# Ten chained transformer sublayers on one core: the last two output slots written token half by token half, the next input prepared in tile pairs, and unused matmuls while TensorE waits at each layer boundary

## What is computed

```python
def first_block(x, c, ...):               # sublayers 0 to 3
    for i in range(2):
        shift, scale, gate = ada_modulation(c, ada_w[i, 0], ada_b[i, 0])
        h = x * (1.0 + scale) + shift
        y = windowed_gqa(h, ...) if i == 0 else recurrent_block(h, ...)   # sublayers 0 and 2
        x = layer_norm(DN_ALPHA * x + (1.0 + gate) * y, ln_g[i, 0], ln_b[i, 0])
        shift, scale, gate = ada_modulation(c, ada_w[i, 1], ada_b[i, 1])
        y = sq_relu_mlp(x * (1.0 + scale) + shift, mlp_w1[i], mlp_w2[i])  # sublayers 1 and 3
        x = layer_norm(DN_ALPHA * x + (1.0 + gate) * y, ln_g[i, 1], ln_b[i, 1])

def second_block(x, ...):                 # sublayers 4 to 9
    for i in range(2):
        x = layernorm(DN_ALPHA_2 * x + 0.5 * swiglu(x, ...), ...)         # 4 and 7
        x = layernorm(DN_ALPHA_2 * x + hybrid_mixer(x, ...), ...)         # 5 and 8
        x = layernorm(DN_ALPHA_2 * x + 0.5 * swiglu(x, ...), ...)         # 6 and 9
```

## Time and profile before

| | |
|---|---|
| median of 3 runs | 2590.63 us (2590.12 to 2590.7) |
| the profiled execution | 2592.34 us, its span 2590.5 us |
| mean granted clock of TensorE in the span | 0.937 of full speed |
| PE busy | 2366.5 us, 91% of the span |
| DVE busy | 1616.8 us, 62% |
| ACT busy | 1116.1 us, 43% |
| POOL busy | 337.1 us, 13% |
| chain that ended last | PE 81%, DVE 14%, ACT 3%, issue 1%, DMA 1% |

### The profile page before, as it was taken

How to read it: one execution, slowest core, us unless ns; L and a number is a source line. 1 busy time by engine, 2 the same in 40 slices (tenths; PEclk the granted TensorE clock), 3 DMA queues, 4 the chain that set the end, 5 groups by cost and what they waited for, 6 DMA issues and landing times.

```text
span 2590.5 us, 37359 instructions
## 1 busy us (share of the span) xinstructions
PE 2366.5 (91%) x15755; PEld 2140.7 (83%) x15755; DVE 1616.8 (62%) x1986; ACT 1116.1 (43%) x1452; POOL 337.1 (13%) x299
## 2 busy tenths in 40 slices
PE   4789997886998999999899889989989999888998
PEld 4668887875987998998788789989989978778997
DVE  6977766698556545698444564464467954447554
ACT  2334433685443433465322344343446643234433
POOL 2112213112001100300112020020030002112000
PEclk9879998997999999999888999999999998899999
DMA  9768882332654556544211255545565532013652
GB/s 322 252 200 289 276 266 90 100 97 94 207 184 147 195 179 179 156 148 122 81 50 66 76 169 185 189 163 186 189 145 157 158 103 66 17 50 130 225 182 98
DMA packets 304282, 400.47 MB, mean 155 GB/s; under 512 B 43216, under 2 KB 262970, under 8 KB 304117
## 3 DMA queue, kind: packets, MB, share of 16 engines
q1 hardware_dynamic: 283360, 336.75, 41.0%
q0 software_dynamic: 17504, 57.89, 7.1%
q10 hardware_dynamic: 3252, 3.45, 0.4%
HBM read 393.86 MB, written 4.19 MB: 154 GB/s over the span
## 4 chain that ended last, share of the span: by engine, by line
PE 81%; DVE 14%; ACT 3%; issue 1%; DMA 1%; POOL 0%; SPq 0%; DVEq 0%; ACTq 0%; POOLq 0%
PE tiles L490 16%; PE tiles L491 16%; PE tiles L492 16%; PE y_rows L490 6%; PE y_rows L492 6%; PE y_rows L491 6%; PE tiles L845 2%; DVE weights_lo L1289 2%; PE tiles L859 2%; PE tiles L855 1%; DVE xt_lo L1382 1%; DVE ada_acc L1339 1%; PE tiles L829 1%; DVE ln_stats L1463 1%; PE tiles L556 1%
## 5 line engine op out<-in xcount | busy, mean ns | idle before, releaser
L1289 DVE TENSOR_TENSOR weights_lo<-weights_raw,weights_hi 128x2048 fp32r<-128x2048 f32 (+2 forms) x316 | 736.5, 2336 | 534.7 <-ACT weights_hi L948 534.4
L490 PE MATMUL tiles<-xt_hi,weights_hi 128*128 128x256 f32 (+1 forms) x3216 | 929.1, 289 | 33.8 <-DVE xt_lo L1382 24.7
L491 PE MATMUL tiles<-xt_lo,weights_hi 128*128 128x256 f32 (+1 forms) x3216 | 920.6, 286 | 0.0
L492 PE MATMUL tiles<-xt_hi,weights_lo 128*128 128x256 f32 (+1 forms) x3216 | 919.8, 286 | 0.0
L948 ACT ACTIVATE weights_hi<-weights_raw 128x2048 fp32r<-128x2048 f32 (+2 forms) x316 | 592.9, 1880 | 218.5 <-PE y_rows L492 192.2
L490 PEld LDWEIGHTS tiles<-xt_hi,weights_hi 128*128 128x128 f32 (+1 forms) x3216 | 620.8, 193 | 51.7 <-issue 37.2
L491 PEld LDWEIGHTS tiles<-xt_lo,weights_hi 128*128 128x128 f32 (+1 forms) x3216 | 621.0, 193 | 3.3
L492 PEld LDWEIGHTS tiles<-xt_hi,weights_lo 128*128 128x128 f32 (+1 forms) x3216 | 620.4, 193 | 0.0
L490 PE MATMUL y_rows<-weights_hi,hid_hi 128*128 128x512 f32 x608 | 244.5, 402 | 0.0
L492 PE MATMUL y_rows<-weights_hi,hid_lo 128*128 128x512 f32 x608 | 242.6, 399 | 0.0
L491 PE MATMUL y_rows<-weights_lo,hid_hi 128*128 128x512 f32 x608 | 242.4, 399 | 0.0
(11 more groups left out here) (331 smaller groups left out, 3128.6 us busy)
## 6 DMA issues: line engine op xcount, KB each, us to landing
weights_raw<-in_ffn_w_dram SPq DMA_DIRECT2D x132, 1024.0 KB, 5.1
weights_raw<-in_mlp_w_dram SPq DMA_DIRECT2D x64, 1024.0 KB, 5.5
weights_raw<-in_w_in_dram SPq DMA_DIRECT2D x52, 1024.0 KB, 5.5
ada_ring<-in_ada_w_dram POOLq DMA_DIRECT2D x76, 512.0 KB, 4.9
weights_raw<-in_rnn_w_in_dram SPq DMA_DIRECT2D x16, 768.0 KB, 4.7
ada_ring<-in_ada_w_dram SPq DMA_DIRECT2D x20, 512.0 KB, 7.4
weights_raw<-in_w_in_dram SPq DMA_DIRECT2D x32, 256.0 KB, 4.4
weights_raw<-in_w_branch_a_dram SPq DMA_DIRECT2D x32, 256.0 KB, 4.9
```

The costliest lines, as they stand in the source:

```text
L490: pe.matmul(o, a, c, start=first, stop=False)
L491: pe.matmul(o, a, d, start=False, stop=False)
L492: return pe.matmul(o, b, c, start=False, stop=last)
L1289: dve.tensor_tensor(slot_view(WLO, m, NSPL), slot_view(RAW, m, NRAW), slot_view(WHI, m, NSPL).bitcast(F32), ALU.subtract).then_inc(*inc("l ...
```

## The change

It has five parts. (1) `rows_tail` takes the last two output slots a and b together: first token half 0 of a and of b (then `y_half`), then token half 1, columns 0 to 511, of a and of b (then the new `y_third`), then columns 512 to 1023 of a; then the eight transposes of the next input's token half 0; then the same columns of b. (2) DVE normalises both halves (L1532 of the changed kernel), and takes t=1 in two column parts. ACT only takes the root, with eps as its bias, and DVE the reciprocal. (3) The transposes go into tiles that belong to one token half each, four blocks in one; ACT applies scale and shift to token half 0 (eight instructions of 128x128) while t=1 is still normalised. For t=1, ACT does four blocks and DVE four; `xt_hi` and `xt_lo` are 128x512 for t=0 and 128x256 for t=1. (4) `keep_busy` issues 22 matmuls of 256 columns behind the last real one and 7 behind the last transposes, into a part of Y that has been read; nobody reads their results. (5) POOL's `scaled` waits until the next sublayer's last `xt_lo` is written. Besides, `xt` lies 8 KB higher, over `hid_act` and `hid_val` instead of over `hid_hi` and `hid_lo`. No DMA is added or removed.

```diff
+WARM_ROWS = 22
+WARM_XT = 7
...
-        XTF = put("xt", [P, KC, S], at=hid_at)
+        XTF = put("xt", [P, KC, S], at=hid_at + 8 * KB)
...
+            def rows_part(label, lh, ll, k0, first, last, t, h):
+                n, wh, wl = open_slot(label)
+                for kk in range(2):
+                    xa, xb = lh(k0 + kk)[:, t * P:(t + 1) * P], ll(k0 + kk)[:, t * P:(t + 1) * P]
+                    ins = mm3(Y[:, t, h * 512:(h + 1) * 512], xa, xb, wh[:, kk, h * 512:(h + 1) * 512],
+                              wl[:, kk, h * 512:(h + 1) * 512], first and kk == 0, last and kk == 1)
+                return ins
+            def rows_tail(s, a, b, b_ready):
+                la, lb = a[0], b[0]
+                for h in range(2):
+                    rows_part(*a, False, False, 0, h)
+                b_ready()
+                for h in range(2):
+                    ins = rows_part(*b, False, True, 0, h)
+                ins.then_inc(*inc("y_half", s))
+                rows_part(*a, False, False, 1, 0)
+                rows_part(*b, False, True, 1, 0).then_inc(*inc("y_third", s))
+                rows_part(*a, False, False, 1, 1).then_inc(*inc("rows_done", la))
+                if s + 1 < n_sub:
+                    prep(s + 1, 0)
+                rows_part(*b, False, True, 1, 1).then_inc(*inc("rows_done", lb))
+                if s + 1 < n_sub:
+                    keep_busy(s, b, WARM_ROWS)
+                    prep(s + 1, 1)
+                    keep_busy(s, b, WARM_XT)
+            def keep_busy(s, slot, n):
+                pe.wait_ge(*past("y_free", (s, 0)))
+                x = OH[:, 0, :] if is_mix(s) else slot[1](slot[3])
+                for _ in range(n):
+                    pe.matmul(Y[:, 0, 0:S], x[:, 0:P], x, start=True, stop=True)
...
+            def prep(s, t):
+                if s > 0:
+                    pe.wait_ge(*past(f"xn_ready{t}", (s - 1, t)))
+                else:
+                    pe.wait_ge(*past("x_in"))
+                for g in range(2):
+                    bank = topen(("xt", s, t, g), "AD"[g * t])
+                    for kk in range(4):
+                        k = 4 * g + kk
+                        ins = pe.transpose(bank[:, kk * P:(kk + 1) * P], XN[:, t, k * P:(k + 1) * P], IDN[:, :])
+                    ins.then_inc(*inc("tile_done", ("xt", s, t, g)))
...
+            rows_tail(0, *(((0, "out", i), lambda k: OH[:, k, :], lambda k: OL[:, k, :], 2 * i) for i in (2, 3)), lambda: None)
...
+                if i < n - 1:
+                    pe.wait_ge(*past("hid_ready", (s, i)))
                 if i == 0:
                     y_wait(s)
-                hh, hl = HH[:, i % 2, :], HL[:, i % 2, :]
-                rows_slot((s, "w2", i), lambda k: hh.rearrange("p (a b) -> p a b", a=2)[:, k],
-                          lambda k: hl.rearrange("p (a b) -> p a b", a=2)[:, k], 0, i == 0, i == n - 1, s)
+                if i < n - 2:
+                    rows_slot(*hidden(s, i), i == 0)
+                elif i == n - 1:
+                    rows_tail(s, hidden(s, i - 1), hidden(s, i), lambda: pe.wait_ge(*past("hid_ready", (s, i))))
...
+                        elif g == 7:
+                            rows_tail(s, ((s, "out", 6), lambda k: YH[:, 2, k, :], lambda k: YL[:, 2, k, :], 0),
+                                      ((s, "out", 7), lambda k: YH[:, 3, k, :], lambda k: YL[:, 3, k, :], 0),
+                                      lambda: pe.wait_ge(*past("yl", 7)))
...
+            def modulate(s, t, g, k0, k1):
                 gp, bp = (GP[:, s, :], BP[:, s, :]) if s < 4 else (LN[s - 1][2], LN[s - 1][3])
+                bank = tile(("xt", s, t, g))
+                for k in range(k0, k1):
+                    ins = act.activation(XTF[:, k, t * P:(t + 1) * P], bank[:, k % 4 * P:(k % 4 + 1) * P], ACT.Identity,
+                                         scale=gp[:, k:k + 1], bias=bp[:, k:k + 1])
+                    ins.then_inc(*(inc("free_A", ("xt", s, t, g)) if k % 4 == 3 else inc("xta_part", (s, t, k))))
...
+            def x_hi(s, t, k0, k1, ready):
+                act.wait_ge(*past(*ready))
+                w = XH[:, k0:k1, t * P:(t + 1) * P]
+                act.activation(w, XTF[:, k0:k1, t * P:(t + 1) * P], ACT.Copy).then_inc(*inc("xh_ready", (s, t, k0)))
+            def prep_first(s):
+                for g in range(2):
+                    modulate(s, 0, g, 4 * g, 4 * g + 4)
+            def prep_rest(s):
+                for g in range(2):
+                    x_hi(s, 0, 4 * g, 4 * g + 4, ("free_A", ("xt", s, 0, g)))
+                modulate(s, 1, 0, 0, 2)
+                x_hi(s, 1, 0, 2, ("xta_part", (s, 1, 1)))
+                modulate(s, 1, 0, 2, 4)
+                x_hi(s, 1, 2, 4, ("free_A", ("xt", s, 1, 0)))
+                x_hi(s, 1, 4, 6, ("xtd_part", (s, 1, 5)))
+                x_hi(s, 1, 6, 8, ("free_D", ("xt", s, 1, 1)))
...
-                    act.wait_ge(*past("ln_recip", (s, t)))
-                    act.activation(RV[:, t, 1:2], RV[:, t, 0:1], ACT.Sqrt).then_inc(*inc("ln_rstd", (s, t)))
-                    if t == 0:
-                        act.activation(RV[:, t, 2:3], MV[:, t, 0:1], ACT.Copy, scale=-1.0).then_inc(*inc("ln_minus", s))
-                        act.wait_ge(*past("ln_minus", s))
-                        act.activation(RV[:, t, 3:4], RV[:, t, 2:3], ACT.Identity, scale=RV[:, t, 1:2]).then_inc(*inc("ln_shift", s))
-                        act.wait_ge(*past("ln_shift", s))
-                        act.activation(XN[:, t, :], XN[:, t, :], ACT.Identity, scale=RV[:, t, 1:2], bias=RV[:, t, 3:4]).then_inc(*inc(f"xn_ready{t}", (s, t)))
+                    act.wait_ge(*past("ln_var", (s, t)))
+                    act.activation(RV[:, t, 1:2], MV[:, t, 1:2], ACT.Sqrt, bias=EPS[:, :]).then_inc(*inc("ln_std", (s, t)))
+                    if t == 0 and s + 1 < n_sub:
+                        prep_first(s + 1)
                 if s + 1 < n_sub:
-                    prep(s + 1)
+                    prep_rest(s + 1)
...
+            def x_lo(s, t, k0, k1):
+                dve.wait_ge(*past("xh_ready", (s, t, k0)))
+                w = (slice(None), slice(k0, k1), slice(t * P, (t + 1) * P))
+                ins = dve.tensor_tensor(XL[w], XTF[w], XH[w].bitcast(F32), ALU.subtract)
+                ins.then_inc(*(inc("xl_ready", (s, k0 // 2)) if t else inc("xl_part", (s, k0))))
+                for g in range(2):
+                    x_lo(s, 0, 4 * g, 4 * g + 4)
+                modulate(s, 4, 6)
+                x_lo(s, 1, 0, 2)
+                modulate(s, 6, 8)
+                for k in (2, 4, 6):
+                    x_lo(s, 1, k, k + 2)
...
+            def residual(s, t, c0, c1):
+                x, y = XN[:, t, c0:c1], Y[:, t, c0:c1]
+                last = c1 == D
+                if s < 4:
+                    dve.tensor_tensor(x, y, GATE[:, c0:c1], ALU.mult).then_inc(*(inc("y_free", (s, t)) if last else inc("y_gated", (s, t))))
+                    dve.wait_ge(*past(*(("y_free", (s, t)) if last else ("y_gated", (s, t)))))
+                    chain(dve.tensor_tensor(x, x, XS[:, t, c0:c1], ALU.add))
+                else:
+                    ins = dve.scalar_tensor_tensor(x, y, 1.0 if is_mix(s) else 0.5, XS[:, t, c0:c1], ALU.mult, ALU.add)
+                    if last:
+                        ins.then_inc(*inc("y_free", (s, t)))
+                        dve.wait_ge(*past("y_free", (s, t)))
+                    else:
+                        chain(ins)
+            def variance(s, t):
+                dve.bn_aggr(MV[:, t, :], ST[:, t, :, :].rearrange("p a b -> p (a b)")).then_inc(*inc("ln_var", (s, t)))
+            def scale_rows(s, t):
+                dve.wait_ge(*past("ln_std", (s, t)))
+                chain(dve.reciprocal(RV[:, t, 0:1], RV[:, t, 1:2]))
+                x = XN[:, t, :]
+                if s + 1 < n_sub:
+                    dve.tensor_scalar(x, x, MV[:, t, 0:1], RV[:, t, 0:1], ALU.subtract, ALU.mult).then_inc(*inc(f"xn_ready{t}", (s, t)))
...
+                residual(s, 0, 0, D)
+                for h in range(2):
+                    ins = dve.bn_stats(ST[:, 0, h, :], XN[:, 0, h * 512:(h + 1) * 512])
+                chain(ins)
+                variance(s, 0)
+                scale_rows(s, 0)
+                dve.wait_ge(*past("y_third", s))
+                residual(s, 1, 0, 512)
+                dve.bn_stats(ST[:, 1, 0, :], XN[:, 1, 0:512]).then_inc(*inc("ln_part", s))
+                dve.wait_ge(*past(*y_end[s]))
+                residual(s, 1, 512, D)
+                dve.wait_ge(*past("ln_part", s))
+                chain(dve.bn_stats(ST[:, 1, 1, :], XN[:, 1, 512:D]))
+                variance(s, 1)
+                scale_rows(s, 1)
...
+                pool.wait_ge(*past("xl_ready", (s + 1, 3)))
```

131 lines of the change are left out of this document (39 added, 92 removed).

## The result

The changed kernel took 2544.47 us (median of 4 runs, 2539.72 to 2545.73) against 2590.66 (2590.12 to 2591.29, 4 runs): ratio 0.9818, 95% interval 0.9805 to 0.983. The profiled execution is the fastest of the four, 2539.72 us with a span of 2537.9, so the two traces are 52.6 us apart.

What follows compares the result with a forecast made beforehand. It took PE standing still at sublayer boundaries, in a relay with DVE and POOL, as the bound. Gains 22.5 + 7.5 + 4.5 + 1.2 + 0 + 3.1 = 38.8 us off 2592.3, less 1.7, gave 2552; range 2541 to 2570.

Steps and rivals of the forecast that it cites:

- Boundaries 4 to 8: Five sublayer boundaries without gate: second column slot 4.8 us earlier, 3.5 if the clock falls; 4.5 taken each, 22.5 in all.
- X: End of DVE's second normalisation (xn_ready1) at a boundary, forecast 9.68 us after the half signal without gate, 11.6 with gate.
- H': The changed kernel's half signal (y_half, token half 0 of y complete), forecast 2.80 us earlier than in the kernel before.
- 3 to 4: Boundary with gate between sublayers 3 and 4: second slot from 26.3 to 18.0 us after the old half signal; gain 7.5.
- 2 to 3: Boundary with gate where the last slot waits for the recurrence: second slot from 650.1 to 644.7; gain 4.5 us taken.
- 0 to 1: Boundary with gate where DVE is busy until 166.96, capping the earlier half signal: gain 1.2 us.
- 1 to 2: Boundary with gate: second slot gains 3.8 us undisturbed, but POOL makes the rnn_decay_cols chain up to 9.6 later; 0 taken.
- The end: Stretch after the last half signal, 12.1 us before, forecast to end 9.0 us after the old half signal: gain 3.1.
- The clock falls at every boundary: Rival: TensorE's clock falls at each sublayer boundary, so the gains are only 32 us: 2558 us; chance 0.24.
- POOL gets in first twice: Rival: POOL's instruction starts ahead of the waiting split, 2.4 us later at eight boundaries; gain 15, 2576 us; chance 0.11.
- Unused matmuls don't stream: Rival: the unused matmuls at nine places run spaced wider, gain gone from 0.28 us, about 2640 at 0.48; chance 0.03.
- No change: Rival: something else, SP's loads, bounds the second slot at the boundaries, so nothing is gained; chance 0.02.

Runs made afterwards that it cites:

- a_pad: The changed kernel with one unused tile of 32 bytes a partition ahead of the gate rows and hidden tiles; 2551.51 us, ratio 0.9854.
- a_slot_by_slot: The changed kernel with the last two output slots computed slot by slot again, so y_half comes with 12 matmuls left, not 24; 2579.57 us.
- a_pool_early: The changed kernel with POOL's scaling of x no longer held back until the last xt_lo; 2575.49 us, ratio 0.9935.
- a_decay_early: The changed kernel with the chain on rnn_decay_cols moved from the start of sublayer 2 into four rounds of sublayer 1; 2533.87 us.
- b_pad: The kernel before with one unused tile of 32 bytes a partition ahead of the gate rows and hidden tiles; 2579.56 us, ratio 0.9959.
- a_no_unused: The changed kernel without its unused matmuls (both counts 0); 2564.46 us, ratio 0.9896.
- b_three: The kernel before with POOL's waits, unused matmuls (20, 8 and 12) and the 32-byte tile, without the new order; 2549.64 us, ratio 0.9844.
- a_both: The changed kernel with the rnn_decay_cols chain moved into sublayer 1 and the last modulation-sum reduction behind slot a's first 12 output matmuls; 2531.37 us.
- a_all: a_both with POOL's scaling also held back until DVE has split the second slot's weights; 2518.07 us, ratio 0.9728.

## Why the prediction was right

The mechanism was right at the boundaries from 2 on and at the end, and the gain came out too small by terms that the sum didn't have. That the foreseen terms came to 38.0 for 38.8 is in part luck: four of them missed by +1.4, +0.8, +1.4 and -4.2 us, and these nearly cancel. `a_pad`, the changed kernel without the unforeseen gain of the 32 bytes, took 2551.51 (2548.36 to 2558.93) for the 2552 forecast. Step by step, between the two profiled executions (52.6 us):

- **Boundaries 4 to 8: right.** Forecast X = H' + 9.68, first slot X + 2.65, second X + 9.2. Measured H' + 9.8, X + 2.6, H' + 18.82. With a half signal 2.76 earlier, the gain is 20.84 - 18.82 + 2.76 = 4.8 each, 23.9 in all; 22.5 was taken, as a mean with a fallen clock.
- **3 to 4: right.** Second slot H + 26.3 before, H' + 20.80 after: 8.3, forecast 7.5.
- **2 to 3: right, too small.** The stretch from half signal to half signal fell by 10.7 (201.2 to 190.5). Less 2.8 for the half signal at its end and 16 slots times 0.13, 5.9 is left; forecast 4.5. No first slot was slow. The prediction's own marks, 650.1 and 644.7, are 5.4 apart, where it wrote 5.0; and both slots came later than marked (H + 27.9 before, H' + 21.9 after).
- **0 to 1 and 1 to 2: the mis-sized terms.** Forecast 1.2 and 0, together +1.2. At 0 to 1 the second slot came at 192.39 against 192.48, a gain of 0.1: X was 181.2, where 178.6 was forecast. DVE is busy there, so PE waited 2.80 us ahead of the first transposes, which then took 1.64 us for 1.09; the last six real matmuls stood behind them, and DVE waited 2.12 for y. It is the same wait that `a_slot_by_slot` shows at other boundaries:

```profile
173.35 1.64 PE L617 MATMUL tiles<-ident,x_rows 128*128 128x128 f32 x8 [2.80 <-DVE x_rows L1532]
...
177.47 0.69 DVE L1511 TENSOR_TENSOR x_rows<-y_rows,gate_rows 128x512 f32<-128x512 f32 x1 [2.12 <-PE y_rows L495]
```

  At 1 to 2 the second slot came at 430.12 against 428.78, and the half signal of sublayer 2 at 624.88 against 623.94; without the 2.1 us that the 32 bytes gave in sublayer 1, that is -3.0. The forecast had y_half at 400.3 and it came at 398.35, after the 4 us that it had named: `386.39` below. The failed size was the next step, "its dozen instructions with two inputs now meet POOL's four blocking ones ... I take half". DVE, then POOL, then PE, 1 to 2 in the changed kernel:

```profile
414.51 0.19 DVE L1615 TENSOR_TENSOR rnn_decay_cols<-rnn_decay_cols,rnn_gate_cols 96x32 f32<-96x32 f32 x1
...
417.43 2.06 DVE L1601 TENSOR_TENSOR rnn_decay_cols<-rnn_decay_cols 96x32 f32<-96x32 f32 x1
...
422.45 2.35 DVE L1607 TENSOR_SCALAR rnn_decay_cols<-rnn_decay_cols 96x32 f32<-96x32 f32 x1
...
427.51 0.90 DVE L1618 TENSOR_SCALAR rnn_decay_cols<-rnn_decay_cols 96x32 f32<-96x32 f32 x1
428.32 5.08 DVE L1341 TENSOR_TENSOR weights_lo<-weights_raw,weights_hi 128x1536 fp32r<-128x1536 f32 x3
...
417.05 2.39 POOL L1884 TENSOR_TENSOR x_scaled<-x_scaled,ln_gb_rows 128x1024 f32<-128x1024 f32 x1
...
422.42 2.34 POOL L1882 TENSOR_TENSOR x_scaled<-x_rows,ln_gb_rows 128x1024 f32<-128x1024 f32 x1
...
386.39 3.55 PE L593 MATMUL tiles<-ones,ada_acc 128*128 128x1 f32 x16 [3.94 <-issue]
...
430.12 0.53 PE L493 MATMUL tiles<-xt_hi,weights_hi 128*96 128x256 f32 x1 [9.76 <-DVE weights_lo L1341]
```

  L1601 takes 0.19 us in the kernel before and L1607 0.33 (L1518 and L1524 there), and here 2.06 and 2.35 beside a POOL instruction of 2.4 us. L1607 has a single input, so the prediction's count of those with two was not the right one. The chain took 14.1 us, from 414.31 to 428.41, beyond the 12 that the prediction had set as its mark for being wrong there; before, it took 7.2. So it lost 6.9 us where 9.6 was the most and half of that was taken. That POOL is the cause is shown by `a_pool_early`, where POOL is done with its two-input instructions before the chain begins: it takes 7.4 us there. `a_decay_early` shows the price: without the chain the 11 us are gone.
- **The end: right.** 12.02 us from the half signal for 12.12, plus 2.76: 2.9, forecast 3.1.

These terms sum to 23.9 + 8.3 + 5.9 - 3.0 + 2.9 = 38.0, forecast 38.8. The other 14.6 us weren't in it (the two items below come to 0.8 more):

- **The 32 bytes**, 9.9 us by the slots, 10.9 by `b_pad`. The prediction said that a matmul of an output slot takes 0.234 and took that for both kernels and for all tiles; it holds for the hidden tiles of the kernel before alone.
- **The mixers.** Sublayer 5 gained 5.6 us more than its boundary (472.81 to 462.46, less 2.02 and 2.76), sublayer 8 0.1 less than its boundary. The code of the mixers is the same in both, and their time goes with the granted clock (see the end). The four runs of the changed kernel show it too: the profiled one had a mean clock of 0.958 and the others 0.954, and by the medians the gain is 46.2 us, which leaves nothing for this item beside the 38.0 and the 9.9.

The rivals. *The clock falls at every boundary*: out, the granted clock was 1.00 in every first slot from 4 on; `a_no_unused` shows what kept it, and that this rival is what the change would be without them. The Trainium skill (TensorE: Matmul & The Clock Gate, "Part 4: PE-mode transpose") says that transposes don't count as activity as matmuls do. `a_no_unused` doesn't contradict it: with transposes alone in the gap the first slot was granted 0.50 to 0.74, with 29 matmuls added 1.00. But the transposes fill only 1.1 us of the 5.7 between the last real matmul and the first slot, so it doesn't separate them from an idle PE. *POOL gets in first twice*: out in the changed kernel; `a_pool_early`, which lets POOL in by another way, lost 30 us, where the rival had 24. *Unused matmuls don't stream*: out, 0.12. *No change* is out too.

What the change is made of, with all runs together: POOL's two waits or the unused matmuls alone take 25 us off the kernel before, an unintended shift by 32 bytes 11, all three 41; the new order, on which the prediction spent most of its working, adds 1.6 us per boundary from 4 on. With only the order of the slots undone the changed kernel loses 36, since the parts that are left then stand in each other's way.

## What to carry to other kernels

Where a wait at a boundary is bound by a vector instruction that suddenly takes three times its usual time, look for what the other engine on SBUF runs beside it; holding that engine back by one semaphore may bring half of what a whole rewrite brings (25 of 46 us here). Test the parts of a change alone and added to the old kernel: parts that remove the same collision don't add up, and a tile of a few bytes may be one of the parts. Small work that needs only parameters belongs where its engine has slack, not at the head of a stage.

## What the runs showed of the hardware

- **The place of a matmul's loaded operand within 64 bytes.** With `hid_hi` and `hid_lo` 32 bytes beyond a multiple of 64, 24 matmuls of 512 columns take 5.59 to 5.60 us; at a multiple 5.47. Four traces were on the first side and ten on the other, without exception. Matmuls of 512 columns whose loaded tile never moved (a multiple of 64) took 5.44 us for 24 in the kernel before. Why isn't shown: the records of the loads last 0.19 us on both sides. Only these two places, 0 and 32 bytes, were tried.
- **DVE and POOL.** The Trainium skill (SBUF — State Buffer, "Who interferes with whom") names DVE instructions with two SBUF inputs, and `tensor_scalar` where it runs in one of its two-port modes. The trace agrees that one with a single input can wait: L1607, a `tensor_scalar`, took 2.35 us beside POOL's L1882 (0.33 free); in which mode it ran isn't shown. The section also says that the engine that comes second blocks fully. That holds against POOL's instructions with two inputs, but POOL's one-input instruction of 3.33 us let four `xt_lo` through in 3.34 (2.6 undisturbed, by 1.29 for two).
- **The mixers' time goes with the granted clock.** From half signal to half signal, sublayers 5 and 8, in us: before 472.8 and 468.9, `b_pad` 473.3 and 467.6, `b_three` 464.5 and 464.4, `a_decay_early` 462.9 and 468.0, `a_both` 465.6 and 469.4, `a_all` 462.2 and 462.1. The code of the mixers is the same in all. The granted clock falls there without a boundary (0.87 in `a_all` and in `a_both` between 1200 and 1400 us), and its mean over the whole stretch falls as the times grow: 0.94 at 462.1 and 462.2 (`a_all`), 0.93 at 468.9 (before), 0.92 at 469.4 (`a_both`), 472.8 (before) and 473.3 (`b_pad`). Why it falls lower in one execution than in another stays open. It is up to 11 us, the size of the smaller effects here, and the likely reason why the runs of `a_both` and `b_three` spread by 14 and 18 us.
